# Retention by chunks, its state products inside a projection tile, and attention products in three fp32r parts, in a hybrid decoder step

## The chip, the cores and the metric

The kernel runs on one core of a Trainium2 chip. The metric is the device time of one execution in microseconds, lower is better. The kernel before took 2383.7 us in the median of three runs (2379.57 to 2384.89). The profile comes from one further execution, which took 2381.4 us and whose span is 2379.6 us.

## The reference, cut to what matters

One step of a one-layer decoder on 512 prompt tokens and 8 sample tokens. The width is split in two: 8 heads of attention (keys and values shared by all heads, keys chosen by an indexer) and 8 heads of retention. After them come an output projection and a large MLP. The change touches the two pieces below, for the prompt alone.

```python
# attention, one block of 128 queries; `valid` and the chosen keys are a mask in the kernel
sc = einsum('bqhd,bqkd->bqhk', qq, kg) * ATTN_HEAD_DIM ** -0.5
p = softmax(where(valid, sc, -inf))
out = einsum('bqhk,bqkd->bqhd', p, vg)

# retention, one chunk of n = 128 tokens; R is the state carried from chunk to chunk
def ret_chunk(R, q, k, v, lg):
    decay = where(diff >= 0, exp(diff * lg), 0)
    inner = einsum('bhij,bjhe->bihe', einsum('bihd,bjhd->bhij', q, k) * decay, v)
    cross = einsum('bihd,bhde->bihe', q, R) * exp((i + 1) * lg)
    zeta = exp((n - 1 - i) * lg)
    R_new = exp(n * lg) * R + einsum('bjhd,bjhe,jh->bhde', k, v, zeta)
    return R_new, inner + cross
```

## The kernel before, in words

Everything is held transposed, features on the 128 partitions and the 520 tokens along the row. A projection makes one tile of 128 output features by 520 tokens: 16 blocks of 128 input features, in two units of 8 (`unit`, `tile`, from L637). Weights and activations are split in a high and a low fp32r part, so that each block is three products (high by high, high by low, low by high) on two halves of 260 tokens: 48 matmuls a unit (L647). Plain float32 matmuls are also in use, for the small products.

The engines run programs of their own and meet by semaphores. SP loads the weights, ACT casts them to the high part (`w_hi`, L1070), POOL subtracts to get the low part (`w_lo`, L582), PE multiplies, DVE takes results out of PSUM (accumulator memory). POOL works a few units ahead of PE.

The change lies in the loop over the 8 heads. Each round has four projection tiles: retention values (tile 0), queries (1), keys (2) and gate (3). The attention and retention work of head `i` is written by hand between them on PE:

- in the middle of tile 1 (`values_and_scores`): the values are turned (transposed), and four score blocks `kt,qc` of 128, 256, 384 and 512 keys are made;
- after tile 2: the softmax results `p_h` are turned in 10 blocks; DVE copies them to `pt_h`;
- in the middle of tile 3 (`output_and_decay`): the attention output (`pt_h,vtok`, four matmuls of 512, 384, 256 and 128 columns), the retention scores (`rq,rk`, the same four sizes), and the turned keys;
- after tile 3, in what is called the tail below: the sample products `vbd,ks_tok`, the retention output (`sd_h,vtok_r`, four sizes), the prompt's final state (`vtok_r,ktok`, four of 128 columns), the sample outputs `rq,rs` (eight matmuls of one column), and sums of squares over the features, made by a matmul with a matrix of ones (`rv,ones`, 512 and 8 columns).

Before, the retention is not done chunk by chunk: all 512 by 512 scores of the lower triangle are made and weighed by the decay (L1713).

The small results share four PSUM banks, called `banks`. On PE `fill(e)` gives the bank of the head's result number e, after a wait until result e - 4 has been taken (`s_xd`); on DVE `full(e)` waits until result e is there (`s_xp`). A head has 24 results. The projection tiles have banks of their own, called `product`; a tile may start when the one two tiles back has been taken (`s_evac`).

At the end of a head ACT squares the retention output `ro`, PE sums, ACT takes a square root, and DVE does a Newton step and the gating; this runs beside tile 0 of the next head. In the last head ACT also casts four finished rows of `mix` (the joined head outputs) to `a_hi` right before it squares (L1156, `mixed(0, 4)`), and the output projection follows the loop.

Of the kernel before, what the change touches and what calls it, by code (L numbers as in the profile page):

```python
# [14 lines left out]
P = 128  # L15
D = 2048
KT = D // P
NP_, NS = 512, 8
# [3 lines left out]
NH = 8  # L22
# [39 lines left out]
def unit_of(tile):  # L62

    return 2 * tile
# [59 lines left out]
def build(nc, x_prompt, x_sample, cache_k, cache_v, cache_idx_k, state_ret, page_table, norm1_g, w_in,  # L124
# [3 lines left out]
    with ctx:  # L128
# [72 lines left out]
        for name, shape, dt, nbytes in (  # L201
# [5 lines left out]
            if name == "am":  # L207
                AM_OFFSET = o
            if name == "const":
                assert o >= SMALL + 16384  # L210
# [4 lines left out]
        kit_o = at("kit_o", AM_OFFSET, [P, NP_])  # L215

# [21 lines left out]
        sd_h = at("sd_h", H0, [P, 1280])  # L238
        pt_h = at("pt_h", H0 + 5120, [P, 1280])
# [6 lines left out]
        qc = at("qc", H0 + 15360, [P, NP_])  # L246
# [82 lines left out]
        def pos_stored(pos):  # L329
# [24 lines left out]
         s_th, s_hs, s_head) = (  # L354
# [4 lines left out]
                "ret_sqrt", "head_done"))  # L359
        (s_t1h, s_t1p, s_t1, s_xb, s_n2, s_n2m, s_n2v, s_n2s, s_nf, s_nfm, s_nfv, s_nfs, s_yt,  # L360
         s_yx, s_ye, s_out, s_rn, s_chain) = (
            sem(n) for n in (
                "mixed_hi", "mixed_lo_pool", "mixed_lo", "x_back", "sum2", "sum2_turned", "var2", "sqrt2",
# [271 lines left out]
        def _(pe):  # L635
# [192 lines left out]
            with pe.Fori(0, NH) as i:  # L828
# [5 lines left out]
                e0 = 24 * i  # L834

                def head_tile(u, between=None):
                    tile(m0 + u, TILE_HEAD + u, n0 + 2 * u, unit_of(TILE_HEAD) + 2 * u, between=between)
# [6 lines left out]
                def values_and_scores():  # L844
# [6 lines left out]
                    turn(B[0:NS, fill(1), 0:P], rv[:, NP_:T], P).then_inc(s_xp, 1)  # L851
                    pe.wait_ge(s_qc, i + 1)
                    for b in range(QB):
                        mm(B[:, fill(2 + b), 0:P * (b + 1)], qc[:, b * P:(b + 1) * P], kt[:, 0:P * (b + 1)]
                           ).then_inc(s_xp, 1)

                def output_and_decay():
                    x = fill(10)
                    pe.wait_ge(s_xd, e0 + TAKEN0 + 10)
                    for k in range(QB):  # L860
# [3 lines left out]
                    pe.wait_ge(s_rk, i + 1)  # L864
                    for k in range(QB):
                        mm(B[:, fill(11 + k), 0:NP_ - k * P], rk[:, k * P:(k + 1) * P], rq[:, k * P:NP_]
                           ).then_inc(s_xp, 1)
                    x = fill(15)
# [3 lines left out]
                    turn(B[0:NS, fill(16), 0:P], rk[:, NP_:T], P).then_inc(s_xp, 1)  # L872
# [1242 lines left out]
```

## Time and profile before

| | |
|---|---|
| median of three runs | 2383.7 us |
| the profiled execution | 2381.4 us, span 2379.6 us |
| PE busy | 2319.0 us, 97% of the span |
| DVE busy | 1620.7 us, 68% |
| ACT busy | 912.4 us, 38% |
| POOL busy | 854.7 us, 36% |
| mean granted TensorE clock | 0.989 of full speed |

The busy time of PE is not its speed: matmuls overlap in the records, so a matmul whose row gives 284 ns starts every 120 ns or so. What a product takes is therefore read from the starts of the rows, not from their lengths. A float32 matmul shows as two records in the rows, an fp32r matmul and a turn as one.

### The profile page before, as it was taken

The numbers are of one execution on the slowest core, as the hardware profiler recorded it, in microseconds if no ns is written. First come the engines' busy times: TensorE is split into PE (matmuls) and PEld (weight loads), VectorE is DVE, ScalarE is ACT, GpSimd is POOL, SyncE is SP. The second block draws the span as 40 slices with busy tenths as digits, with TensorE's granted clock in tenths as the row PEclk, the third lists the DMA queues.
The fourth block names the chain that finished last, engine by engine and source line by source line (L and its number), as shares of the span: only waits on it lengthen the run. The fifth ranks groups of instructions, "written<-read, shape, count | busy, mean of one in ns | idle before, by whom it ended". The sixth has DMA issues, their size and how long they took to land.

```text
span 2379.6 us, 46108 instructions
## 1 busy us (share of the span) xinstructions
PE 2319.0 (97%) x18386; PEld 2244.1 (94%) x18386; DVE 1620.7 (68%) x2452; ACT 912.4 (38%) x1180; POOL 854.7 (36%) x355
## 2 busy tenths in 40 slices
PE   8999999999999999999999999999899999999997
PEld 7979899999999899989999999999899999999996
DVE  5358725555555533478888899888877777777775
ACT  5241222222222433355555555555433333333344
POOL 2522322232333444333333333333333333333354
PEclk9999999999999999999999999999999999999998
DMA  6533323333333353425555555566875567655621
GB/s 222 131 80 91 95 63 86 94 85 94 83 81 86 103 178 115 129 74 185 201 199 187 188 191 185 189 201 201 300 256 199 189 210 246 209 185 197 225 97 72
DMA packets 349079, 368.77 MB, mean 155 GB/s; under 512 B 16818, under 2 KB 301682, under 8 KB 348018
## 3 DMA queue, kind: packets, MB, share of 16 engines
q1 hardware_dynamic: 336866, 352.16, 46.5%
q10 hardware_dynamic: 12064, 14.53, 1.7%
q8 instruction: 105, 1.72, 0.3%
q14 instruction: 44, 0.36, 0.1%
HBM read 288.85 MB, written 77.80 MB: 154 GB/s over the span
## 4 chain that ended last, share of the span: by engine, by line
PE 67%; DVE 20%; issue 7%; ACT 4%; DMA 1%; POOL 0%; ACTq 0%; SPq 0%; DVEq 0%; POOLq 0%
PE product L647 30%; PE product L936 29%; DVE banks L1867 7%; PE banks L678 6%; DVE h_lo L1908 4%; ACT w_hi L1249 3%; DVE h_f L1897 2%; DVE w_lo L1873 2%; PE banks L675 1%; DVE c_b L1832 1%; DMA x_in<-in_x_prompt_dram 1%; DVE h_f L1899 1%; DMA w_raw<-in_w_in_dram 1%; ACT h_f L1073 1%; DVE a_lo L1456 0%
## 5 line engine op out<-in xcount | busy, mean ns | idle before, releaser
L615 POOL TENSOR_TENSOR w_lo<-raw,w_hi 128x1024 fp32r<-128x1024 f32 x193 | 495.2, 2566 | 825.5 <-ACT w_hi L1249 825.3
L936 PE MATMUL product<-s_up,w_hi 128*128 128x260 f32 x3600 | 657.4, 284 | 9.0 <-DVE w_lo L1873 5.4
L936 PE MATMUL product<-s_dn,w_hi 128*128 128x260 f32 x3584 | 652.4, 284 | 8.8 <-DVE xr L1975 3.3
L936 PEld LDWEIGHTS product<-s_up,w_hi 128*128 128x128 f32 x3600 | 557.1, 189 | 15.2 <-DVE w_lo L1873 10.5
L936 PEld LDWEIGHTS product<-s_dn,w_hi 128*128 128x128 f32 x3584 | 552.6, 188 | 12.7 <-issue 4.9
L582 POOL TENSOR_TENSOR w_lo<-w_raw,w_hi 128x1024 fp32r<-128x1024 f32 (+1 forms) x134 | 321.8, 2404 | 659.2 <-ACT w_hi L1070 659.0
L936 PE MATMUL product<-s_up,w_lo 128*128 128x260 f32 x1800 | 510.1, 283 | 0.0
L936 PE MATMUL product<-s_dn,w_lo 128*128 128x260 f32 x1792 | 506.9, 283 | 0.0
L647 PE MATMUL product<-a_hi,w_hi 128*128 128x260 f32 (+1 forms) x2144 | 439.6, 286 | 8.9 <-DVE a_lo L1456 3.9
L647 PE MATMUL product<-a_hi,w_lo 128*128 128x260 f32 (+1 forms) x2144 | 433.5, 284 | 0.0
L647 PE MATMUL product<-a_lo,w_hi 128*128 128x260 f32 (+1 forms) x2144 | 432.7, 283 | 0.0
L1249 ACT CAST w_hi<-banks 128x1024 fp32r<-128x1024 f32 x244 | 247.1, 1013 | 452.4 <-DVE banks L1867 342.4
L1873 DVE TENSOR_TENSOR w_lo<-banks,w_hi 128x1024 fp32r<-128x1024 f32 x244 | 297.9, 1221 | 105.5 <-ACT w_hi L1249 105.5
L1070 ACT CAST w_hi<-w_raw 128x1024 fp32r<-128x1024 f32 (+1 forms) x134 | 139.6, 1043 | 555.7 <-PE product L647 414.7
L647 PEld LDWEIGHTS product<-a_hi,w_hi 128*128 128x128 f32 (+1 forms) x2144 | 331.4, 189 | 16.5 <-issue 8.1
L936 PEld LDWEIGHTS product<-s_up,w_lo 128*128 128x128 f32 x1800 | 340.2, 189 | 0.0
L936 PEld LDWEIGHTS product<-s_dn,w_lo 128*128 128x128 f32 x1792 | 336.8, 188 | 0.0
L647 PEld LDWEIGHTS product<-a_hi,w_lo 128*128 128x128 f32 (+1 forms) x2144 | 331.4, 189 | 0.0
L647 PEld LDWEIGHTS product<-a_lo,w_hi 128*128 128x128 f32 (+1 forms) x2144 | 330.3, 188 | 0.0
L1249 ACT CAST w_hi<-raw 128x1024 fp32r<-128x1024 f32 x193 | 203.2, 1053 | 187.5 <-PE product L936 170.3
L1975 DVE TENSOR_TENSOR xr<-xr,product 128x260 f32<-128x260 f32 x416 | 174.5, 420 | 122.7 <-PE product L936 121.2
L1867 DVE TENSOR_TENSOR banks<-raw 128x1024 f32<-128x1024 f32 x118 | 191.9, 1626 | 0.0
(289 smaller groups left out, 1875.6 us busy)
## 6 DMA issues: line engine op xcount, KB each, us to landing
raw<-in_w_up_dram SPq DMA_DIRECT2D x64, 1024.0 KB, 8.4
raw<-in_w_down_dram SPq DMA_DIRECT2D x64, 1024.0 KB, 5.7
s_dn<-hidden_combinations SPq DMA_DIRECT2D x112, 520.0 KB, 8.5
w_raw<-in_w_in_dram SPq DMA_DIRECT2D x100, 512.0 KB, 3.9
hidden_combinations<-h_hi SPq DMA_DIRECT2D x31, 910.0 KB, 3.8
hidden_combinations<-h_lo SPq DMA_DIRECT2D x31, 910.0 KB, 6.6
w_raw<-in_w_out_dram SPq DMA_DIRECT2D x32, 512.0 KB, 4.0
x_transposed<-xr ACTq DMA_DIRECT2D x2, 2080.0 KB, 7.6
```

What stands on the lines that cost most here:

```text
L582: nc.gpsimd.tensor_tensor(w_lo[:, slot, :, 0:cols], w_raw[:, raw, :, 0:cols], w_hi[:, slot, :, 0:cols].bitcast(F32), ALU.subtract).then_in ...
L615: nc.gpsimd.tensor_tensor(ring(w_lo, g, n), block_of(g, i, j), ring(w_hi, g, n).bitcast(F32), ALU.subtract).then_inc(s_lo, 1)
L647: last_mm = nc.tensor.matmul(out[:, half, :], w[:, slot, k, 0:cols], a[:, k0 + k, half * HT:(half + 1) * HT], start=(first and k == 0 and ...
L678: return nc.tensor.matmul(out, lhsT, rhs, start=start, stop=stop, skip_group_check=True)
L936: mm_last = nc.tensor.matmul(out, w[:, k, col:col + P], s[:, h, k, :], start=(first and k == 0 and part == 0), stop=(last and k == kn - 1 ...
L1070: nc.scalar.copy(w_hi[:, n % RING, :, 0:cols], w_raw[:, n % 2, :, 0:cols]).then_inc(s_hi, 1)
L1249: nc.scalar.copy(ring(w_hi, g, n), x).then_inc(s_hi, 1)
L1867: v.tensor_tensor(out, x, y, ALU.add).then_inc(s_t, 1)
L1873: v.tensor_tensor(ring(w_lo, g, n), sums_in(g, (k + 1) % 2), ring(w_hi, g, n).bitcast(F32), ALU.subtract).then_inc(s_lt, 1)
L1897: v.tensor_tensor(h_f[:, 5, :], h_f[:, 0, :], a21[:, :], ALU.subtract)
L1908: v.tensor_tensor(low[:, :, :], h_f[:, :, :], high[:, :, :].bitcast(F32), ALU.subtract).then_inc(s_hl, 1)
L1975: ins = v.tensor_tensor(acc, acc, part, op)
```

## The change

Four things are changed in the head loop, and one before it.

1. The attention scores and outputs are each made of three fp32r matmuls (high by high, high by low, low by high) instead of one float32 matmul. The parts of the shared keys and values are made once, before the loop (four DVE operations, of which the last two wait until the values have been stored). The parts of the queries are made by DVE in each head (`qc`, `qc_lo`). Of the turned probabilities ACT makes the high part from PSUM and DVE the low part (`pt_lo`); before, DVE made one copy.
2. Retention is done by chunks: four score blocks of 128 columns in one bank, one decay multiplication, and for chunks 1 to 3 a second matmul with the state carried so far (`carry`) on decayed queries (`rqd`).
3. The products for the states are no longer in the tail. They are kept apart by chunk, and go in before block 14 of the 16 of tile 3 (`partial_states`), with the sample products `vbd,ks_tok`. DVE then makes the carried states and the final state from them.
4. On DVE the sample states `rs` are updated before the gate tile is taken, not after. A head now has 20 results in the banks. The small sum of the sample squares goes to the bank of the sample outputs.

```diff
@@ PE
                     for b in range(QB):
-                        mm(B[:, fill(2 + b), 0:P * (b + 1)], qc[:, b * P:(b + 1) * P], kt[:, 0:P * (b + 1)]
-                           ).then_inc(s_xp, 1)
+                        x, rows_, keys = fill(2 + b), slice(b * P, (b + 1) * P), slice(0, P * (b + 1))
+                        for part, (q, k) in enumerate(((qc, kt_hi), (qc_lo, kt_hi), (qc, kt_lo))):
+                            last = mm(B[:, x, keys], q[:, rows_], k[:, keys], start=(part == 0), stop=(part == 2))
+                        last.then_inc(s_xp, 1)
...
                     for k in range(QB):
-                        last = mm(B[:, x, k * P:NP_], vtok[:, k, :], pt_h[:, KOFF[k]:KOFF[k] + NP_ - k * P],
-                                  start=(k == 0), stop=(k == QB - 1))
+                        for part, (values, probs) in enumerate(((vtok_hi, pt_h), (vtok_hi, pt_lo), (vtok_lo, pt_h))):
+                            last = mm(B[:, x, k * P:NP_], values[:, k, :], probs[:, keys],
+                                      start=(k == 0 and part == 0), stop=(k == QB - 1 and part == 2))
...
                     for k in range(QB):
-                        mm(B[:, fill(11 + k), 0:NP_ - k * P], rk[:, k * P:(k + 1) * P], rq[:, k * P:NP_]
-                           ).then_inc(s_xp, 1)
+                        last = mm(B[:, x, k * P:(k + 1) * P], rk[:, k * P:(k + 1) * P], rq[:, k * P:(k + 1) * P])
+                    last.then_inc(s_xp, 1)
...
+                def partial_states(k):
+                    if k != 14:
+                        return
+                    x = fill(14)
+                    pe.wait_ge(s_xd, e0 + TAKEN0 + 14)
+                    for c in range(QB):
+                        last = mm(B[:, x, c * P:(c + 1) * P], ktok[:, c, :], vtok_r[:, c, :])
+                    last.then_inc(s_xp, 1)
+                    pe.wait_ge(s_vbd, i + 1)
+                    for j in range(2):
+                        mm(B[:, fill(15 + j), :], ks_tok[:, :], vbd[:, 4 * j:4 * j + 4, :]).then_inc(s_xp, 1)
...
+                head_tile(3, between=output_and_decay, ready=partial_states)
+                x = fill(17)
                 for k in range(QB):
-                    last = mm(B[:, x, k * P:NP_], vtok_r[:, k, :], sd_h[:, KOFF[k]:KOFF[k] + NP_ - k * P],
-                              start=(k == 0), stop=(k == QB - 1))
+                    out = B[:, x, k * P:(k + 1) * P]
+                    last = mm(out, vtok_r[:, k, :], sd_h[:, k * P:(k + 1) * P], stop=(k == 0))
+                    if k:
+                        if k == 1:
+                            pe.wait_ge(s_cq, i + 1)
+                        pe.wait_ge(s_sc1, 3 * i + k)
+                        last = mm(out, carry[:, k - 1, :], rqd[:, (k - 1) * P:k * P], start=False)
@@ ACT
                 high(base + 5, i8)
+                for k in range(QB):
+                    n = NP_ - k * P
+                    act.wait_ge(s_xp, 20 * i + 7 + k)
+                    nc.scalar.copy(pt_h[:, KOFF[k]:KOFF[k] + n], B[:, (6 + k) % 4, 0:n]).then_inc(s_pth, 1)
                 act.wait_ge(s_rq, i + 1)
@@ DVE
+                full(9)
                 for k in range(QB):
-                    n = NP_ - k * P
-                    v.tensor_copy(pt_h[:, KOFF[k]:KOFF[k] + n], B[:, full(6 + k), 0:n]).then_inc(s_xd, 1)
+                    n = slice(KOFF[k], KOFF[k] + NP_ - k * P)
+                    dve.wait_ge(s_pth, 4 * i + k + 1)
+                    v.tensor_tensor(pt_lo[:, n], B[:, (6 + k) % 4, 0:NP_ - k * P], pt_h[:, n].bitcast(F32),
+                                    ALU.subtract).then_inc(s_xd, 1)
...
-                for k in range(QB):
-                    v.tensor_tensor(sd_h[:, KOFF[k]:KOFF[k] + n], B[:, full(11 + k), 0:n], dh[:, 0:n], ALU.mult
-                                    ).then_inc(s_xd, 1)
+                v.tensor_tensor(sd_h[:, :].rearrange("p (k d) -> p k d", d=P),
+                                B[:, full(11), :].rearrange("p (k d) -> p k d", d=P),
+                                dh[:, 0:P].unsqueeze(1).to_broadcast([P, QB, P]), ALU.mult).then_inc(s_xd, 1)
...
-                scaled(halves(rg[:, :]), m0 + 3, (TILE_HEAD + 1) % 2)
+                v.tensor_tensor(rqd[:, :], rq[:, P:NP_], dh[:, P:NP_], ALU.mult).then_inc(s_cq, 1)
+                x = full(14)
+                v.tensor_scalar(carry[:, 0, :], B[:, x, 0:P], st[:, 45:46], None, ALU.mult).then_inc(s_sc1, 1)
+                for k in range(1, QB - 1):
+                    dve.wait_ge(s_sc1, 3 * i + k)
+                    v.scalar_tensor_tensor(out=carry[:, k, :], in0=B[:, x, k * P:(k + 1) * P], scalar=st[:, 45:46],
+                                           in1=carry[:, k - 1, :], op0=ALU.mult, op1=ALU.add).then_inc(s_sc1, 1)
+                dve.wait_ge(s_sc1, 3 * i + 3)
+                v.scalar_tensor_tensor(out=rst[:, :], in0=carry[:, QB - 2, :], scalar=st[:, 37:38],
+                                       in1=B[:, x, (QB - 1) * P:NP_], op0=ALU.mult, op1=ALU.add).then_inc(s_xd, 1)
                 dve.wait_ge(s_rs, 16 * i + 16)
...
+                scaled(halves(rg[:, :]), m0 + 3, (TILE_HEAD + 1) % 2)
+                v.tensor_copy(ro[:, 0:NP_], B[:, full(17), :]).then_inc(s_xd, 1)
```

Two places of the order matter most. The first is PE's tail, from the end of tile 3 to the sum of squares. Before it stands so:

```order
L647 MATMUL product<-a_hi,w_lo 128x260 x2
L841 REGISTER_ALU [waits values_diagonal]
...
L678 MATMUL banks<-vbd,ks_tok 128x512 [waits head_bank_taken]
...
L678 MATMUL banks<-sd_h,vtok_r 128x512 [waits head_bank_taken]
L678 MATMUL banks<-sd_h,vtok_r 128x384
L678 MATMUL banks<-sd_h,vtok_r 128x256
L678 MATMUL banks<-sd_h,vtok_r 128x128
...
L678 MATMUL banks<-vtok_r,ktok 128x128 x3
...
L678 MATMUL banks<-rq,rs 128x1 x7
...
L678 MATMUL banks<-rv,ones 128x512 [waits head_bank_taken,ret_squared]
```

In the changed kernel the same stretch, from the last blocks of tile 3 on (`vtok_r,ktok` are the state products, now in the middle of tile 3's second unit, and `rqd,carry` the products with the carried states):

```order
L692 MATMUL banks<-vtok_r,ktok 128x128 [waits head_bank_taken]
L692 MATMUL banks<-vtok_r,ktok 128x128 x3
L856 REGISTER_ALU [waits values_diagonal]
...
L692 MATMUL banks<-vbd,ks_tok 128x512 [waits head_bank_taken]
L661 MATMUL product<-a_hi,w_hi 128x260 x2
...
L692 MATMUL banks<-sd_h,vtok_r 128x128
L926 ISA [waits ret_q_decayed]
L692 MATMUL banks<-rqd,carry 128x128 [waits states_carried]
L692 MATMUL banks<-sd_h,vtok_r 128x128
...
L692 MATMUL banks<-rqd,carry 128x128 [waits states_carried]
...
L692 MATMUL banks<-rq,rs 128x1 x7
...
L692 MATMUL banks<-rv,ones 128x512 [waits head_bank_taken]
```

The sample products and the state products have moved ahead of the last two blocks of tile 3 (six matmuls each), and the sums of squares are the last thing in the tail as before, behind the sample outputs `rq,rs`.

The second place is DVE, from the sample values `vbd` to the retention output, where `rg` is the gate tile, `rs` the sample states and `ro` the retention output. Before:

```order
L1719 TENSOR_TENSOR vbd<-vs_tok,const 72x1024
...
L1476 TENSOR_TENSOR rg<-product,rb 128x520 [waits weights_used]
...
L1725 SCALAR_TENSOR_TENSOR rs<-rs,st,banks 128x512 [waits head_bank_full]
...
L1725 SCALAR_TENSOR_TENSOR rs<-rs,st,banks 128x512 [waits head_bank_full]
...
L1728 COPY ro<-banks 128x512 [waits head_bank_full]
...
L1729 COPY rst<-banks 128x128 [waits head_bank_full]
...
L1730 COPY ro<-banks 128x8 [waits head_bank_full]
```

And in the changed kernel:

```order
L1769 TENSOR_TENSOR vbd<-vs_tok,const 72x1024
L1771 TENSOR_TENSOR rqd<-rq,dh 128x384
...
L1773 TENSOR_SCALAR carry<-banks,st 128x128 [waits head_bank_full]
...
L1776 SCALAR_TENSOR_TENSOR carry<-banks,st,carry 128x128 [waits states_carried]
...
L1776 SCALAR_TENSOR_TENSOR carry<-banks,st,carry 128x128 [waits states_carried]
...
L1779 SCALAR_TENSOR_TENSOR rst<-carry,st,banks 128x128 [waits states_carried]
...
L1784 SCALAR_TENSOR_TENSOR rs<-rs,st,banks 128x512 [waits head_bank_full]
...
L1784 SCALAR_TENSOR_TENSOR rs<-rs,st,banks 128x512 [waits head_bank_full]
...
L1512 TENSOR_TENSOR rg<-product,rb 128x520 [waits weights_used]
...
L1788 COPY ro<-banks 128x512 [waits head_bank_full]
```

The gate tile was first in DVE's queue at the end of tile 3; now five small operations and the two updates of the sample states stand ahead of it, and the copy of `ro` stands behind it.

## Rows read from the trace of the kernel before

**Rows 1.** The page, busy time and share of the span of each engine.
```profile
PE 2319.0 (97%) x18386; PEld 2244.1 (94%) x18386; DVE 1620.7 (68%) x2452; ACT 912.4 (38%) x1180; POOL 854.7 (36%) x355
```

**Rows 2.** Chain of waits, 430 to 520 us: start us, us, what, matmul records.
```profile
449.69 17.57 PE product L647 x144
...
468.49 1.92 PE banks L678 x4
...
494.59 4.31 PE banks L678 x16
498.90 0.55 PE banks L675 x5
...
505.23 6.28 PE banks L678 x38
...
511.57 8.54 PE product L647 x69
```

**Rows 3.** PE's timeline, a tail: start us, us, engine, line, operation, output<-inputs, records.
```profile
505.06 0.62 PE L678 MATMUL banks<-vbd,ks_tok 72*128 72x512 f32 x2
505.52 2.32 PE L678 MATMUL banks<-sd_h,vtok_r 128*128 128x512 f32 x8
507.68 1.06 PE L678 MATMUL banks<-vtok_r,ktok 128*128 128x128 f32 x8
508.57 1.84 PE L678 MATMUL banks<-rq,rs 128*128 128x1 f32 x16
510.28 1.23 PE L678 MATMUL banks<-rv,ones 128*128 128x512 f32 x4
```

**Rows 4.** Timeline of PE's weight loads at the scores, in brackets the wait.
```profile
467.54 0.53 PEld L678 LDWEIGHTS banks<-kt,qc 128*128 128x128 f32 x4
468.49 0.30 PEld L678 LDWEIGHTS banks<-kt,qc 128*128 128x128 f32 x2 [0.42 <-DVE vtok_r L1688]
469.28 0.30 PEld L678 LDWEIGHTS banks<-kt,qc 128*128 128x128 f32 x2 [0.50 <-DVE vs_tok L1660]
```

**Rows 5.** Timeline of DVE, ACT and POOL in a tail, in brackets the wait.
```profile
443.95 1.40 DVE L1725 SCALAR_TENSOR_TENSOR rs<-rs,st,banks 128x512 f32<-128x512 f32 x2
...
444.45 2.36 POOL L582 TENSOR_TENSOR w_lo<-w_raw,w_hi 128x1024 fp32r<-128x1024 f32 x1 [8.21 <-ACT w_hi L1070]
...
445.95 0.69 DVE L1728 COPY ro<-banks 128x512 f32<-128x512 f32 x1 [0.60 <-PE banks L678]
...
446.67 0.63 ACT L1073 ACTIVATE rv<-ro 128x512 f32<-128x512 f32 x1 [1.76 <-DVE ro L1728]
446.84 0.29 DVE L1729 COPY rst<-banks 128x128 f32<-128x128 f32 x1 [0.20 <-PE banks L678]
...
448.52 0.17 DVE L1730 COPY ro<-banks 128x8 f32<-128x8 f32 x1 [1.39 <-PE banks L678]
```

**Rows 6.** Timeline of ACT, POOL and DVE in tile 3, up to `vbd`.
```profile
488.82 1.19 ACT L1165 COPY t<-product 64x520 f32<-64x520 f32 x2
488.88 2.40 POOL L582 TENSOR_TENSOR w_lo<-w_raw,w_hi 128x1024 fp32r<-128x1024 f32 x1 [3.29 <-ACT w_hi L1070]
...
490.67 1.17 DVE L1679 SCALAR_TENSOR_TENSOR t<-t,cs 128x520 f32<-128x520 f32 x1
...
500.89 1.22 DVE L1719 TENSOR_TENSOR vbd<-vs_tok,const 72x1024 fp32r<-72x1024 f32 x1
```

**Rows 7.** Timeline of ACT and PE in the last head's tail.
```profile
815.98 0.62 PE L678 MATMUL banks<-vbd,ks_tok 72*128 72x512 f32 x2
...
817.72 2.19 ACT L1156 CAST a_hi<-mix 128x520 fp32r<-128x520 f32 x4
...
821.19 1.23 PE L678 MATMUL banks<-rv,ones 128*128 128x512 f32 x4
```

**Rows 8.** Busy us (count) of each engine by stretch, then the granted clock of PE.
```profile
573.00:574.00 1.00, 0.92 (x7) 0.79 (x7) 0.70 (x3) 0.40 (x1) 0.00 (x0) 0.95 0.23 66
574.00:575.00 1.00, 1.00 (x6) 1.00 (x6) 0.67 (x2) 0.99 (x2) 0.00 (x0) 0.50 0.83 269
```

More of the change, by code:

```diff
@@ L829, in _, with head_tile @@
                 m0, n0 = TILE_HEAD + 4 * i, unit_of(TILE_HEAD) + 8 * i
-                e0 = 24 * i
-                def head_tile(u, between=None):
-                    tile(m0 + u, TILE_HEAD + u, n0 + 2 * u, unit_of(TILE_HEAD) + 2 * u, between=between)
+                e0 = 20 * i
+                def head_tile(u, between=None, ready=None):
+                    tile(m0 + u, TILE_HEAD + u, n0 + 2 * u, unit_of(TILE_HEAD) + 2 * u, between=between,
+                         ready=ready)
                 def fill(e):
@@ L883, in _ @@
                     last.then_inc(s_xp, 1)
[L884 to L900 removed]
+                head_tile(3, between=output_and_decay, ready=partial_states)
+                x = fill(17)
+                for k in range(QB):
+                    out = B[:, x, k * P:(k + 1) * P]
[5 more added lines that the diff above has]
+                        last = mm(out, carry[:, k - 1, :], rqd[:, (k - 1) * P:k * P], start=False)
+                last.then_inc(s_xp, 1)
+                x = fill(18)
+                pe.wait_ge(s_xd, e0 + TAKEN0 + 17)
                 for b in range(NS):
@@ L1196, in act_head @@
                     mixed(4, 5)
[L1197 removed]
+                act.wait_ge(s_xd, 20 * i + TAKEN0 + 20)
+                act.wait_ge(s_vt, i + 1)
                 act_fn(rk[:, :], rv[:, :], ACT.Sqrt).then_inc(s_hs, 1)
@@ L1661, in split_thirds @@
                 return last
+            v.tensor_copy(kt_hi[:, :], kt[:, 0:NP_]).then_inc(s_kv, 1)
+            dve.wait_ge(s_kv, 1)
+            v.tensor_tensor(kt_lo[:, :], kt[:, 0:NP_], kt_hi[:, :].bitcast(F32), ALU.subtract).then_inc(s_kv, 1)
+            dve.wait_ge(s_kvo, 64)
+            v.tensor_copy(vtok_hi[:, :, :], vtok[:, :, :]).then_inc(s_kv, 1)
+            dve.wait_ge(s_kv, 3)
+            v.tensor_tensor(vtok_lo[:, :, :], vtok[:, :, :], vtok_hi[:, :, :].bitcast(F32), ALU.subtract
+                            ).then_inc(s_kv, 1)
             v.memset(ks_tok[:, :].bitcast(F32), 0.0)
             step(v.memset(vs_tok[:, :].bitcast(F32), 0.0))
-            with step.loop(NH, 14) as i:
-                m0, e0 = TILE_HEAD + 4 * i, 24 * i
+            with step.loop(NH, 15) as i:
+                m0, e0 = TILE_HEAD + 4 * i, 20 * i
                 def full(e):
@@ L1685, in _ @@
                 step(v.tensor_copy(st[:, 41:42], gamma[:, one(i)]))
-                v.tensor_copy(qc[:, :], row(qa, i)[:, 0:NP_]).then_inc(s_qc, 1)
+                step(v.reciprocal(st[:, 45:46], st[:, 37:38]))
+                v.tensor_copy(qc[:, :], row(qa, i)[:, 0:NP_]).then_inc(s_qch, 1)
+                dve.wait_ge(s_qch, i + 1)
+                v.tensor_tensor(qc_lo[:, :], row(qa, i)[:, 0:NP_], qc[:, :].bitcast(F32), ALU.subtract
+                                ).then_inc(s_qc, 1)
                 scaled(halves(rv[:, :]), m0, TILE_HEAD % 2)
```

79 lines of the change are left out of this document (41 added, 38 removed).

## The prediction, made before the changed kernel was run

> **What bounds the kernel now.** I read the page first: PE is busy for 97% of the span and DVE for 68% [rows 1]. Then the chain of waits over one head, because the whole change lies in the eight rounds of that loop. The chain is PE alone: from tile 0's start at 449.69 to the next one at 511.57, 61.88 us a head, and none of the listed pieces is another engine's [rows 2]. So a microsecond taken from PE's stream is a microsecond of the kernel, as long as no other engine becomes late; and the work put on ACT and DVE is free only as far as it is ready when PE comes to it. Starts in PE's timeline give what each product takes [rows 3], the waits before the weight loads show the two places where PE already stands still for DVE [rows 4], and DVE's, ACT's and POOL's timelines give the durations for the new chains [rows 5, 6].
>
> **The unit prices.** The projection has 144 matmuls of 260 columns in 17.57 us [rows 2], 0.122 us each. The fp32r pair of 512 columns runs from 505.06 to 505.52, 0.23 us each [rows 3]. The float32 product of four sizes (1280 columns) runs from 505.52 to 507.68, 2.16 us; four float32 matmuls of 128 columns from 507.68 to 508.57, 0.89 us, 0.222 each, 0.111 a record; one-column matmuls 16 records from 508.57 to 510.28, 0.107 a record [rows 3]. That last row says that a record with almost no columns still takes 0.107 us: the weights have to be loaded. I take that as the floor of a 128-column fp32r matmul: 0.113 us.
>
> **Part 1, attention in three parts.** No row shows fp32r under 260 columns. My values for one fp32r matmul: 128 columns 0.113 (the floor), 256 0.120 (as 260), 384 0.172 (between 260 and 512), 512 0.23. Three of each: 3 x 0.635 = 1.90 us, against 2.16 before. Output: -0.26 us a head. By size it is a loss at 128 columns (0.34 against 0.22) and a gain from 256 up. From above, a 128-column one could cost what a float32 one does, 0.222: +0.33 us a head on the output. From below 0.056, half a float32 record (128 columns at the rate of the 512): -0.17.
> The Trainium skill ("TensorE: Matmul & The Clock Gate", LDWEIGHTS) has a load of P columns at P/1.2 ns, 107 ns for 128, which speaks against cutting into 128-column pieces; the one-column row agrees (107). The same page (Back-to-back issue gap) has N/2.4 + 2.5 ns for an isolated matmul, 56 ns at 128 columns; an estimate by that alone makes the three-part set 1.63 us and the kernel about 2 us faster than I say. At 260 columns it has 111 ns against 122 measured, so I stay with the rows.
> The scores gain less, because PE stands there for DVE: 0.42 us for the values and 0.50 for `vs_tok` before the last, 512-column block, whose load starts at 469.28 [rows 4]. These ends don't move, and the first three blocks lie before them, so only the last block counts: four passes of 512 columns take 2.16 x 512/1280 = 0.86 us, three fp32r 0.69: -0.17 us a head.
> The new operations beside it: ACT's four copies to the high part go ahead of the half swap (488.82) [rows 6]. ACT takes 0.63 for 512 columns [rows 5], about 1.9 for the four; the swap then ends near 491.9. DVE's four subtractions follow the copies and end near 491.6, the rotation of the keys ends near 494.6. PE wants the probabilities at 494.4 and the rotated keys behind the 1.9 us of the output, at 496.3. Both hidden, with 1.7 us to spare at the narrower place. The query split (0.7 us more on DVE at a head's start) lies ahead of taking tile 0, and PE wants that tile only a unit later, 48 x 0.122 = 5.9 us. The splits before the loop have the whole of tile 0, 11.7 us.
>
> **Part 2, retention by chunks.** The scores: 0.89 for 2.16, -1.27 us a head. The second half: before, output 2.16 and state 0.89, 3.05 together; after, state products 0.89 and seven matmuls of 128 columns, 1.55, together 2.44: -0.61 us a head. On DVE one multiplication of 512 columns (0.69) takes the place of four.
>
> **Part 3, the states inside tile 3.** Taking them out of the tail makes nothing cheaper on PE; it changes who is late. PE reaches block 14 some 4.3 us (36 matmuls) after the turned keys, 7.6 us after the start of the output. DVE has by then, counted from that start: the attention output 2.1 to 2.8, the decay to 3.7, `ktok` to 4.4, three small splits to 5.3, `vbd` (1.22 [rows 6]) to 6.6, `rqd` to 7.2. So PE finds everything there, with 1 us to spare. One more change between fp32r and float32 is new: I give it 0.1 us, half of what lies between the sums' work (510.28 plus 0.86 and 0.21) and tile 0's start at 511.57 [rows 2, 3]. Bounds 0 to 0.3.
>
> **Part 4, the tail.** Let S be the start of the state products. They end at S + 0.89, `vbd` at S + 1.35, tile 3 at S + 2.9. DVE: three carries and the final state at 0.29 each (a 128-column copy [rows 5]) with some 0.17 between, to S + 2.8; two updates of `rs`, 1.40 [rows 5], to S + 4.15; the gate tile, 0.70, to S + 4.85; the copy of `ro`, 0.69, to S + 5.5. ACT: tanh to S + 5.5, square 0.63 to S + 6.2. PE: seven matmuls to S + 4.45, the sample outputs 1.71 to S + 6.16, and then it wants the squares. So the square, which was ready 1 us early (446.67 + 0.63 [rows 5], against 510.28 less a period [rows 3]), is now just late: +0.1 us a head. Bounds -0 and +0.7.
>
> **The sum for heads 1 to 7.** -0.26 - 0.17 - 1.27 - 0.61 + 0.1 + 0.1 = -2.1 us; times 7: -14.8 us. Every period should go from 61.9 to 59.8.
>
> **The last head.** ACT has four casts, 2.19 us, between tanh and square [rows 7]. Before they lay beside 6.3 us of tail. Now tanh ends 2.6 us after tile 3, the casts at 4.8, the square at 5.5, where PE is there at 3.3. The sum of squares starts 5.5 after the tile's end; before, it was 5.2 (821.19 less 815.98, where the sample products begin [rows 7]). The tail gains nothing, and what the middle gains (1.27 + 0.26 + 0.17) is used up by the state products moved into it (1.35) and the 0.1. About 0 for this head, where 2.1 would be expected.
>
> **The total.** 2381.4 - 14.8 = 2366.6 us for the profiled execution. The median lies 2.3 above that execution, which gives 2368.9. I take 2368. Everything after the loop stays bound by PE and only starts earlier.
>
> **The rivals.**
> *The clock.* After one of the eight tails the granted clock fell from 1.00 to 0.50 (2.4 to 1.2 GHz) for some 3.4 us, behind the one-column matmuls and the sums [rows 8]; half of that, 1.7 us, is lost. For it: the tail keeps its thinnest piece and gets a short stand still. Against: its other pieces are as dense as they were, and seven tails went by undisturbed. If it happens after most tails, six more, +10 us: 2378, a gain of about 0.2%. Chance 8%.
> *Small fp32r matmuls at float32's price.* If both 128 and 256 columns, the sizes below any row, cost as float32 (0.222 and 0.43), one set takes 3 x (0.222 + 0.43 + 0.172 + 0.23) = 3.16 us. The output loses 1.0 instead of gaining 0.26; at the scores the first three blocks now pass the waits and the loss is about 0.55. The head's gain falls to 0.1 us, the last head loses 1.5: 2382, no change. For it: no row excludes it. Against: the rate is flat between 260 and 512. Chance 6%. With 128 columns alone at that price it is 2.6 us: 2371, within my range.
> *Slower: the gate tile and the copy of `ro` behind POOL.* A DVE operation on two SBUF operands stands still while POOL works: the rotation's second step, 1.17 us for 520 columns, ends 0.56 after POOL's `w_lo` does (490.67 + 1.17 against 488.88 + 2.40) [rows 6]. POOL's `w_lo` runs from 1.3 to 3.7 us after tile 3's end (444.45 to 446.81 [rows 5], the end being 505.06 less a period). Before, the gate tile was done by then; now it lies in the middle of it (from 1.25 to 1.95). If it is held till POOL ends, it ends at 4.3, the square at 5.8, and PE waits 2.5 us in each head: 7 x 2.4 and as much in the last, +19 us: 2387, slower. It decides from a delay of 2.1 us a head. Against: two updates of `rs`, which like the gate tile read one PSUM and one SBUF operand, ran in the same POOL operation at 0.70 us each (1.40 for two, POOL from 444.45) [rows 5]. Chance 4%.
> *The move backfires at block 14.* If DVE is some 2 us late with `vbd`, PE stands in the middle of tile 3. POOL's hold could put 1.7 us on `vbd` or `rqd`, of which 1 us is covered: +0.7 a head, 2374. Chance 8%.
>
> **How the numbers follow.** The forecast 2368 has 70%, with an own range of 2363 to 2374 from the bounds above (-1.4 and +2.6 for small fp32r matmuls, up to +4 for the tail's wait, two clock falls of 1.7 either way, the run's own spread). The others: clock 8, block 14 8, small matmuls 6, POOL 4, and 4 left for what I don't see, on the slow side. The range for 8 in 10 is 2361 to 2376. Within 0.2% (4.8 us) of 2383.7 is what a measurement of this kernel cannot tell from no change: faster, under 2378.9, 0.85; same 0.09; slower 0.06.
>
> **What would show it.** The chain should still be PE alone, with starts of tile 0 59.8 us apart; 0.89 us between the first retention score and the turned keys; 1.9 us for the twelve output matmuls (2.3 would mean float32's price at 128 columns); no wait at block 14; the sum of squares starting 3.3 to 3.4 us after tile 3's end in seven heads and about 5.5 in the last, with the wait put down to ACT. I am wrong if PE's product starts in the tail or at block 14 are more than 0.5 us later than this, or if the clock falls after more than two tails.

## The result, and the profile after

The changed kernel took 2364.03 us (median of four runs, 2361.38 to 2365.37); the kernel before, run beside it, 2382.83 us (2379.57 to 2384.89). The ratio is 0.9922, with a 95% interval of 0.991 to 0.9935: 18.8 us faster, a little under 0.8%. The forecast was 2368, the range 2361 to 2376. The profiled execution took 2365.37 us (span 2363.6, mean granted clock 0.986, against 2379.6 and 0.989 before).

The page of the kernel after, busy time of each engine (it answers to [rows 1]):

```profile
PE 2304.8 (98%) x18498; PEld 2253.6 (95%) x18498; DVE 1630.9 (69%) x2480; ACT 922.2 (39%) x1212; POOL 853.5 (36%) x355
```

PE has 112 more records and is busy for 14 us less; DVE is busy for 10 us more. Next the chain of waits of the kernel after over one period and a half (start us, us, what, matmul records), which answers to [rows 2]:

```profile
428.58 5.78 PE product L661 x48
434.37 2.80 PE banks L692 x20
...
437.71 4.34 PE product L661 x36
442.05 1.35 PE banks L692 x10
443.40 1.44 PE product L661 x12
444.84 4.33 PE banks L692 x34
...
449.19 19.07 PE product L661 x144
...
510.24 9.87 PE product L661 x80
```

Over this stretch it is still PE alone. Output and retention scores take 2.80 us where they took 4.31, the tail's chain piece 4.33 where it took 6.28, and the state products stand inside tile 3 as 1.35 (442.05). From 449.19 to 510.24 there are 61.05 us, but tile 0 took 19.07 there instead of 17.57: the clock had fallen. Undisturbed periods, as from 510.24 to the next tile 0 at 569.73, are 59.5 us; before they were 61.9. That is 2.4 us a head, where I said 2.1.

The sum of the profiled execution: from the first tile 0 to the end of the last sum of squares it was 498.1 us (324.16 to 822.27) and is 482.9 (327.67 to 810.59), 15.2 less. Seven heads at 2.4 would be 16.8 and the last head's middle 0.4, 17.2 together; 2.0 are missing, nearly all of it the clock's part: the last sum of squares ran at half clock (1.1) and more of the first tile did (0.8). The loop began 3.5 us later, with more half clock ahead of it. What follows it took 4.3 less (1557.3 and 1553.0 us), though its code is the same; in the profiled execution of experiment 9 the same code took 1556.5, so I don't count these 4.3 as the change's. The two profiled executions differ by 16.0 us and the medians by 18.8; no row shows where the other 2.8 come from.

The prices of the new products stand in PE's timeline of the kernel after (start us, duration us, engine, line, operation, output<-inputs, records; durations overlap, so the starts are read):

```profile
434.20 0.39 PE L692 MATMUL banks<-pt_h,vtok_hi 128*128 128x512 f32 x1
...
434.90 0.34 PE L692 MATMUL banks<-pt_h,vtok_hi 128*128 128x384 f32 x1
...
435.43 0.28 PE L692 MATMUL banks<-pt_h,vtok_hi 128*128 128x256 f32 x1
...
435.78 0.22 PE L692 MATMUL banks<-pt_h,vtok_hi 128*128 128x128 f32 x1
...
436.06 1.10 PE L692 MATMUL banks<-rq,rk 128*128 128x128 f32 x8
```

512 columns take 0.235 us each (434.20 to 434.90 for three), 384 take 0.177, 256 take 0.117 and 128 take 0.093 (the starts of this last group are uneven; experiment 7 prices it better); the set is 1.86 us, where I had 1.90 and float32 took 2.16 [rows 3].

The tail of the kernel after, DVE, ACT, POOL and PE in one timeline (in brackets the wait), which answers to [rows 5]:

```profile
444.40 1.40 DVE L1784 SCALAR_TENSOR_TENSOR rs<-rs,st,banks 128x512 f32<-128x512 f32 x2
...
444.68 0.60 PE L692 MATMUL banks<-sd_h,vtok_r 128*128 128x128 f32 x4
...
445.72 0.69 DVE L1512 TENSOR_TENSOR rg<-product,rb 128x520 f32<-128x520 f32 x1
...
446.00 2.36 POOL L596 TENSOR_TENSOR w_lo<-w_raw,w_hi 128x1024 fp32r<-128x1024 f32 x1 [8.02 <-ACT w_hi L1101]
...
446.24 1.84 PE L692 MATMUL banks<-rq,rs 128*128 128x1 f32 x16
...
447.17 0.63 ACT L1104 ACTIVATE rv<-ro 128x512 f32<-128x512 f32 x1
...
447.95 1.23 PE L692 MATMUL banks<-rv,ones 128*128 128x512 f32 x4
```

Tile 3 ends at 444.68. The square is done at 447.80 and PE takes it at 447.95, without a wait: 3.27 us after tile 3's end, as forecast (3.3 to 3.4). The copy of `ro` (446.44) lies wholly beside POOL's operation, the gate tile with its last 0.4 us, and each takes 0.69 us, so POOL holds neither.

Behind this tail the clock fell. The stretches of the kernel after (busy us and count of each engine, then PE's granted clock), as [rows 8] of before:

```profile
449.00:450.00 1.00, 0.98 (x7) 0.89 (x6) 0.91 (x3) 0.07 (x1) 0.00 (x0) 0.73 0.35 102
450.00:451.00 1.00, 1.00 (x7) 1.00 (x6) 0.46 (x1) 1.00 (x1) 0.00 (x0) 0.50 0.89 291
```

About 3.4 us at 0.50 (1.2 of 2.4 GHz), of which half, 1.7, would be lost; the period shows 1.5 of it (61.05 against 59.5). It happened after one of the seven tails, as before.

### The profile page after: what moved, and what is told of

It is laid out like the page before. It is cut to its first block, busy times and chain, and to the rows that moved or that the text cites. A ratio compares the mean times of both kernels' runs of the same rounds, so it can differ in the third digit from the quotient of the medians.

```text
span 2363.6 us, 46420 instructions
## 1 busy us (share of the span) xinstructions
PE 2304.8 (98%) x18498; PEld 2253.6 (95%) x18498; DVE 1630.9 (69%) x2480; ACT 922.2 (39%) x1212; POOL 853.5 (36%) x355
## 4 chain that ended last, share of the span: by engine, by line
PE 67%; DVE 21%; issue 7%; ACT 4%; DMA 1%; POOL 0%; DVEq 0%; SPq 0%; ACTq 0%
PE product L661 32%; PE product L967 28%; DVE banks L1927 7%; PE banks L692 5%; DVE h_lo L1968 4%; ACT w_hi L1285 3%; DVE w_lo L1933 2%; DVE h_f L1957 2%; PE banks L689 1%; DVE c_b L1892 1%; DMA x_in<-in_x_prompt_dram 1%; DVE h_f L1959 1%; ACT h_f L1104 1%; DVE s_up L1874 1%; DVE h_f L1958 0%
```

## The experiments

All edits are to the kernel after. "Seven tails" are those of heads 1 to 7. The kernel before, run beside them, had medians of 2381.4 to 2382.6 us.

**1. Attention in float32 (part 1 undone).**

```
- for part, (q, k) in enumerate(((qc, kt_hi), (qc_lo, kt_hi), (qc, kt_lo))):
-     last = mm(B[:, x, keys], q[:, rows_], k[:, keys], start=(part == 0), stop=(part == 2))
+ mm(B[:, x, keys], qc[:, rows_], kt[:, keys]).then_inc(s_xp, 1)
  (the output product likewise, with vtok and pt_h in float32; ACT's copies and DVE's splits go)
```

> The changed kernel with the attention scores and outputs as single float32 matmuls again (no parts of keys, values, queries and probabilities, no ACT copies). My theory: part 1 is worth 0.26 us a head on the output and 0.17 on the scores, so the head's period goes from 59.5 us to 59.9 and the kernel is 3 to 4 us slower than the changed one (about 2367). Rival, small fp32r pieces are dear: no change or a gain. Rival, the extra gain that I didn't foresee comes from this part: 6 us or more slower.

Measured: 2367.69 us (2364.76 to 2375.96), ratio 0.9946 [0.9931, 0.9961]. Its chain of waits:

```profile
446.48 17.51 PE product L661 x144
...
491.30 3.05 PE banks L692 x16
...
506.36 8.75 PE product L661 x71
```

A period of 59.88 to 59.9 us, 0.4 more than after: output and retention scores 3.05 against 2.80 (0.25; I had 0.26), the rest at the scores. Part 1, undone alone, is worth 0.4 us a head; the other 2.0 are with parts 2 to 4.

**2. State products in the tail (the move undone).**

```
- head_tile(3, between=output_and_decay, ready=partial_states)
+ head_tile(3, between=output_and_decay)
+ partial_states()
```

> The changed kernel with the state products and the sample products behind tile 3 again, everything else as it is. Theory: the move makes nothing cheaper on PE but hides DVE's chain (carries, final state, sample states, gate tile, copy of ro) behind two blocks of tile 3. Without it PE reaches the sample outputs 2.9 us after tile 3's end, the sample states are ready at 4.0, the squares at 6.1 where PE is there at 5.8: 1.5 us a head more than the changed kernel, period 61.0, some 11 us slower in all (about 2375), about what the kernel before took less the attention part and a third of the chunking. Rival, the move is neutral because DVE is not late: within 2 us of the changed kernel.

Measured: 2386.92 us (2378.58 to 2393.5), ratio 1.0026 [1.0013, 1.004]: slower than the kernel before, 22 us above after, where I expected half of that. PE in two of its tails, and its waits from 380 to 800 us (us in total, times, longest):

```profile
571.14 1.95 PE L692 MATMUL banks<-rq,rs 128*128 128x1 f32 x16 [0.89 <-DVE rs L1783]
...
631.79 1.96 PE L692 MATMUL banks<-rq,rs 128*128 128x1 f32 x16 [0.89 <-DVE rs L1783]
```

```profile
PE banks L692 <- DVE rs L1783: 6.2, 7, 0.9
```

The one-column products, which need the updated `rs`, stand 0.9 us for DVE in every tail. And the clock fell after five of seven tails. A stretch of another of its tails:

```profile
511.00:512.00 1.00, 1.00 (x2) 0.48 (x3) 0.14 (x1) 0.21 (x1) 0.00 (x0) 0.50 0.00 0
```

From one tail to the next, a period without a fall is 60.65 us (571.14 to 631.79), 1.1 above after, of which the stand is 0.9; I had expected 61.0. A period with a fall is 62.2 (508.94 to 571.14). So seven heads cost about 8 us by the waits. The profiled execution was the fastest of the seven, only 13.2 us above the profiled one of after; in the others the clock was lower still. Over all runs the mean granted clock was 0.9816, against 0.9870 in after, and 0.0054 of 2385 us is 13 us: an estimate, which with the 8 makes 21 of the 22.9.

**3. Gate tile first in the tail (part 4's order undone).**

```
+ scaled(halves(rg[:, :]), m0 + 3, (TILE_HEAD + 1) % 2)
  for j in range(2):
      (the two updates of rs)
- scaled(halves(rg[:, :]), m0 + 3, (TILE_HEAD + 1) % 2)
```

> The changed kernel with the gate tile taken before the two updates of the sample states, as in the kernel before. Theory: DVE then waits with the updates for tile 3's end (gate tile to 0.9 us after it, updates to 2.3), and PE, which comes to the sample outputs 1.56 us after tile 3, stands 0.8 us in each head: period 60.3, some 5 to 6 us slower (about 2369.5). Rival, the tail of the changed kernel is bound by the squares on ACT: tanh is done earlier here, so the squares come no later and nothing changes.

Measured: 2379.31 us (2376.18 to 2384.71, 12 runs), ratio 0.9991 [0.9982, 0.9999]. 15 us given back, not 5 or 6. PE's product in the first tail, then the timeline of the second and its clock:

```profile
384.83 1.95 PE L692 MATMUL banks<-rq,rs 128*128 128x1 f32 x16 [0.54 <-DVE rs L1785]
...
443.09 0.70 DVE L1512 TENSOR_TENSOR rg<-product,rb 128x520 f32<-128x520 f32 x1 [0.40 <-PE product L661]
443.70 1.40 DVE L1785 SCALAR_TENSOR_TENSOR rs<-rs,st,banks 128x512 f32<-128x512 f32 x2
...
445.15 2.17 PE L692 MATMUL banks<-rq,rs 128*128 128x1 f32 x16 [0.54 <-DVE rs L1785]
```

```profile
445.00:446.00 1.00, 0.84 (x8) 0.85 (x8) 0.70 (x2) 0.27 (x1) 1.00 (x1) 1.00 0.00 0
...
447.00:448.00 1.00, 1.00 (x3) 0.67 (x4) 0.17 (x1) 0.21 (x1) 0.00 (x0) 0.50 0.00 0
```

The gate tile waits 0.40 us for PE and then runs ahead of the updates; the one-column products stand 0.54 us, and 1.6 us later the clock goes to half. It fell after six of seven tails, and once stayed down for twice the 3.4 us. The one period before any of these falls is 60.32 us (384.83 to 445.15), just the 60.3 that I had expected, 0.8 more than after. The periods that hold one fall are 61.7 to 61.8. So what I missed is the clock. 15.3 us are 2.2 a head: with the falls behind it, a stand of half a microsecond costs four times its length. All runs have that clock, not only the profiled one: 0.9833 in the mean against 0.9870, some 9 us by the same estimate.

**4. Both undone (states in the tail, gate tile first).** Edits 2 and 3 together: with them nothing of the new order is left, only the cheaper products.

> The changed kernel without part 3: state and sample products behind tile 3 and the gate tile first in DVE's queue there, as before the change. Chunking and the three-part products stay. Theory: PE stands about 1.0 us for the sample states and nothing or 0.2 for the squares, as with the late gate tile, and the clock falls after most tails (1.7 us each). Period 61.1 without such a fall; 2380 to 2388 in all, so that the whole gain of parts 1 and 2 is eaten. Rival, with the gate tile first the chain is short enough: under 2372.

Measured: 2381.67 us (2379.61 to 2388.28, 11 runs), ratio 1.0004 [0.9995, 1.0013]. The wait from 380 to 800 us:

```profile
PE banks L692 <- DVE rs L1784: 6.3, 7, 0.9
```

0.9 us in each tail, and the clock fell after all seven, so that there is no period without a fall to read; with one it is 62.1 us. The mean clock of all runs was 0.9824. Without the new order the whole gain of the cheaper products is gone: what PE saves turns into a wait for DVE and a slower clock.

**5. The last head: a quarter of the casts ahead of the squares, the rest behind.**

```
- mixed(0, 4)
+ mixed(0, 1)
  (the squares)
+ if last: mixed(1, 4)
```

> The changed kernel with one cast of mix ahead of the squares in the last head and the other three behind them. Theory: PE stood 1.75 us there and its clock fell to half for 3.4 us behind it; with one cast the wait is 0.6 us, the clock stays, POOL (busy until 3.7 us after the tile) starts its eight subtractions no later, and DVE's subtractions start 2 to 3 us earlier, which takes away the 1.8 us wait of the output projection for a_lo. 2 us faster than the changed kernel (about 2362). Rival: the output projection is bound by POOL's eight subtractions, and nothing is gained: within 0.5 us. The seven other heads must not move.

Measured: 2363.51 us (2358.77 to 2368.01), ratio 0.9925 [0.9911, 0.9939], the same as after; the times alone cannot tell a gain of 2 us from one of 0.5. PE in its last tail, then its waits from 330 to 860 us:

```profile
804.67 1.24 PE L692 MATMUL banks<-rv,ones 128*128 128x512 f32 x4 [0.17 <-ACT rv L1104]
```

```profile
PE product L661 <- POOL a_lo L619: 3.5, 8, 0.7
```

The stand for ACT goes from 1.8 us to 0.2, and no clock fall follows. But PE then reaches the out projection sooner and waits 3.5 us, in eight pieces, for POOL's subtractions for `a_lo`. The last wait of PE for DVE's `a_lo` ends 2.33 us earlier than in after (827.61, 829.94), but the tail's one-column products start 2.19 us earlier too (802.65, 804.84), so the edit gained 0.1 there. The rival was right: the wait moves to the next engine.

**6. An extra copy of a 260-column PSUM block on DVE, ahead of the gate tile.**

```
+ v.tensor_copy(qc[:, 0:HT], G[:, 2 * ((TILE_HEAD + 1) % 2), 0:HT])
  scaled(halves(rg[:, :]), m0 + 3, (TILE_HEAD + 1) % 2)
```

> The changed kernel with one extra copy on DVE (260 columns out of PSUM, 0.42 us, its result is used by nobody) ahead of the gate tile. It doses the delay of the squares. In the changed kernel the square ends 0.15 us before PE wants it, so PE should stand 0.25 to 0.3 us in each tail. Theory A, only the wait counts: period 59.5 to 59.8, 2 to 2.5 us slower than the changed kernel. Theory B, what made the two earlier undone orders so slow is the granted clock, which falls after a tail in which PE stands still: then more than one of the seven tails should be followed by half clock, at 1.7 us each, and the kernel is 5 to 12 us slower. I hold B.

Measured: 2367.46 us (2364.26 to 2368.61), ratio 0.9935 [0.9921, 0.9949]. Its chain:

```profile
570.32 17.37 PE product L661 x144
...
629.83 10.20 PE product L661 x84
```

59.51 us, as after, though the copy takes 0.42 us of DVE. The sum of squares starts 0.2 us later, but tile 0 behind it takes 17.37 instead of 17.55, so that the period gives it back. I had thought that the tail had nearly no slack; a delay of 0.4 us costs nothing in the period. The median is 3.4 us above after all the same. One more fall (1.5 us) and a longer stand in the last head (2.09 us for 1.75) are part of it; the rest no row shows. Two of seven tails were followed by half clock, with only 0.2 us of stand ahead of the squares, so this run does not decide between theories A and B.

**7. Output pieces of 64 columns.** The last 128-column piece of the output as two of 64, six matmuls for three.

> The changed kernel with the 128-column piece of the attention output made as two pieces of 64 columns, so six fp32r matmuls for three. Theory: a small fp32r matmul costs its weight load, 0.107 to 0.113 us, whatever its columns; the set takes 0.32 us more (2.18 for 1.86). Rival, it costs its columns: the set stays within 0.05 us.

Measured: 2371.53 us, one run. Its chain:

```profile
571.62 17.57 PE product L661 x144
...
616.34 3.14 PE banks L692 x23
...
631.44 8.62 PE product L661 x70
```

Period 59.82, 0.3 more; the piece of output and scores 3.14 us against 2.80, 0.34 for three more matmuls: 0.11 each. A matmul of 64 columns costs what one of 128 does, and a one-column record 0.107 us [rows 3]: the columns don't set the price there. That it is the weight load is the reading that fits; no run took the load away.

**8. The block of `vs_tok` given back after two of its three reads** (the third copy reads the SBUF copy).

```
- split_thirds(vs_tok, B[0:NS, full(1), 0:P], ("hi", "lo", "hi")).then_inc(s_xd, 1)
+ step(v.tensor_copy(vs_tok[0:NS, :], x))
+ v.tensor_tensor(vs_tok[THIRDS[1]:...], x, vs_tok[0:NS, :]..., ALU.subtract).then_inc(s_xd, 1)
+ step(v.tensor_copy(vs_tok[THIRDS[2]:...], vs_tok[0:NS, :]...))
```

> The changed kernel, and on DVE the bank with the sample values is given back after two of its three reads; the third copy reads the SBUF result. Theory: PE stands 0.32 us for this bank before the 512-column score block; the release comes 0.3 us earlier, of which the end of the block before allows 0.15 to 0.2. Period 59.5 to 59.3, 1 to 1.5 us faster than the changed kernel. Rival, the next wait (the bank of the first result) takes its place and nothing moves.

Measured: 2360.89 us (2358.96 to 2365.84), ratio 0.9913 [0.99, 0.9927]; the periods are 59.2 us. Its chain over one head:

```profile
403.61 2.15 PE banks L692 x12
405.76 17.27 PE product L661 x144
...
444.72 17.55 PE product L661 x144
...
464.96 5.13 PE product L661 x43
```

The first tile behind the scores starts 59.20 us later (405.76, 464.96) and the scores are 2.15 us, where after they were 1.46 and 0.96 with a wait of 0.32. That wait is gone and 0.3 us a head is won, some 2 us in seven heads; the wait of 0.19 us one block earlier stays. By the medians this is 3 us under after, but the runs' own spread is as large.

**9. A stand of 0.7 us elsewhere.** PE waits behind tile 2 of each head for an extra DVE copy that can start only when that tile is done.

```
  head_tile(2)
+ pe.wait_ge(s_stand, i + 1)
```

> The changed kernel with a stand of PE of about 0.7 us in each head, but away from the tail: after tile 2 PE waits until DVE has copied 260 columns out of that tile's PSUM (a result nobody uses). It tells apart what lowers the clock in the orders whose tails have a wait of 0.5 to 0.9 us. Theory: a short stand does it only beside the thin one-column matmuls of the tail; here the seven heads cost 0.7 us each and no more of them than one or two are followed by half clock: about 2370. Rival: any stand of that length does it; then most heads show half clock behind tile 2, 1.7 us each, and the kernel takes about 2380.

Measured: 2374.67 us (2368.18 to 2375.27), ratio 0.9958 [0.9944, 0.9973]. The stand, and the clock behind it:

```profile
548.30 1.30 PE L689 MATMUL banks<-const,p_h 128*128 128x128 f32 x10 [0.71 <-DVE qc L1755]
```

```profile
549.00:550.00 1.00, 1.00 (x11) 1.00 (x10) 0.32 (x1) 1.00 (x3) 1.00 (x1) 1.00 0.00 0
```

The clock stayed at 1.00 behind all of these stands; it fell after two of the seven tails. The period without a fall is 60.45 us, 0.95 more. So a stand of 0.7 us among dense matmuls costs its length and some 0.2; one of 0.54 us beside the one-column matmuls cost 1.7 us beyond its length (experiment 3). That period is nearly the 60.32 us of experiment 3, so a longer way from tail to tail isn't what lowers the clock there. The median is 10.6 us above after, of which eight periods give 7.6; in the profiled execution the code behind the loop took 3.5 us more.

**10. Scores from the largest block down, with edit 8.**

```
- for b in range(QB):
+ for j, b in enumerate(reversed(range(QB))):
```

> The early release of the sample values' bank, and the four score blocks in the order 512, 384, 256, 128 keys instead of 128 to 512 (on PE, DVE and ACT alike). Theory: the two waits of PE for DVE there (0.19 and 0.32 us a head in the changed kernel) lie behind the small blocks because these are too short to cover DVE's copy; with the big blocks first both waits are covered, the stretch falls from 2.43 to about 1.9 us, the period from 59.5 to 58.95, and the kernel is 4 to 5 us faster than the changed one, some 2 faster than the early release alone. Rival: DVE's softmax steps on the big blocks come late for the third and fourth and the waits only move: the same as the early release alone.

Measured: 2363.06 us (2358.29 to 2365.55), ratio 0.992 [0.9907, 0.9934]. Its chain:

```profile
403.90 1.87 PE banks L692 x12
405.77 17.37 PE product L661 x144
...
444.83 5.19 PE product L661 x41
```

The twelve score matmuls take 1.87 us, with no wait left. The period is 59.05 us; of the 0.28 won at the scores against edit 8, the next 144 matmuls give back 0.1. The medians don't tell this kernel from after or from edit 8: it is 1 us under after, where I expected 4 to 5. By the period it is the best of all, 2.9 us a head under the kernel before.

## Why the prediction was right, point by point

**PE alone is the bound, so its saving is the kernel's.** Right, but under a condition that I gave too little weight (below). That the loop's sums nearly agree, -14.8 forecast and -15.2 in the profile, is partly luck: each of seven heads gained 0.3 more than I said (2 us), and the half clock in the first tile and in the last sum of squares took 1.9 back.

**Part 1.** Output forecast -0.26 a head, measured 0.25 by experiment 1. Scores -0.17: the stretch went from 2.60 to 2.43 us, as forecast, because only the block behind the last wait counted. The waits at the scores became 0.19 and 0.32 us [rows 4: 0.42 and 0.50]; the ends did not move. The price at 128 columns (0.113 us) holds: experiment 7 gives 0.11. The formula for an isolated matmul in the Trainium skill ("TensorE: Matmul & The Clock Gate", Back-to-back issue gap) would have made the output set 1.63 us, an estimate; 1.86 were measured, and the measurement decides. With these 1.86 the rival of small matmuls at float32's price falls too, since it has 3.16.

**Part 2.** Forecast -1.27 at the retention scores; with the output -1.53, measured 4.31 - 2.80 = 1.51.

**Parts 2 to 4, the tail.** This is the term of the sum that was mis-sized. Forecast, the state products' 1.4 in tile 3 included: -0.61 + 0.1 + 0.1 = -0.41 a head. Measured, from tile 3's end to the next tile 0: 6.51 us before (505.06 to 511.57 [rows 2, 3]) and 4.51 after (444.68 to 449.19), with 1.35 more in tile 3: -0.65. Neither of my two tenths came. The second unit of tile 3 with the states inside is 4.34 + 1.35 + 1.44 = 7.13 us, and 48 matmuls without them are 5.78 in the same chain (428.58), so nothing is paid for changing from fp32r to float32 and back. And the square was in time, since DVE's operations followed one another more closely than the 0.17 us that I put between them: the gate tile ended at 446.41, 1.73 after tile 3's end, where I had 1.95. The rest of the 2.4, 0.06 a head, lies in the projection's tiles.

**The last head.** Forecast 0, with the sum of squares about 5.5 us after the tile's end, put down to ACT. Measured, in PE's timeline of the kernel after:

```profile
808.44 2.29 PE L692 MATMUL banks<-rv,ones 128*128 128x512 f32 x4 [1.75 <-ACT rv L1104]
```

It starts 5.16 us after the tile's end at 803.28. Up to that end the head is 0.4 us shorter than before, which its middle gives. The clock fell at this stand, and the sum of squares took 2.15 us instead of 1.08: from tile 0 to its end the head is 0.6 longer. That one us is on the path, since DVE's normalization starts from that sum. So the forecast of 0 was 0.6 us off, by a clock fall that it did not have.

**The rivals.** *The gate tile behind POOL*: it did not happen, by the tail shown above. *Block 14 backfires*: it did not; `vbd` was done at 440.5 and `rqd` at 441.0, PE came at 441.89 without a wait. *The clock*: in this kernel no, one fall in seven tails as before. But it is the closest of the rivals, and I gave it 8% by the wrong argument, that the tail's pieces are as dense as they were. What the runs show to matter is whether PE stands beside the one-column products. The stands there and the falls behind them, over all kernels, with the mean granted clock of all runs of each:

```
kernel                       stand at rq,rs   falls in 7 tails   mean clock
before, after                0                1, 1               0.988, 0.987
1, 5, 6, 7, 8, 10            0                2, 1, 2, 0, 1, 0   0.986 to 0.988
9 (0.7 us elsewhere)         0                2                  0.987
3 gate tile first            0.54             6                  0.983
2 states in the tail         0.89             5                  0.982
4 both                       0.9              7                  0.982
```

Experiment 3 is the cleanest of them: PE's own order is that of after, and only the stand is new. The eighth tail says the same. In ten of the twelve kernels PE stands there for half a microsecond or more, before `rq,rs` or between them and the sums of squares, 1.75 us in after, and the clock fell there in all ten; in the other two, before and experiment 5, it stands 0 and 0.17 us and the clock stayed.

Without the move of the state products and the order of the tail the kernel is 17.6 us slower (experiment 4 against after), nearly the whole 18.8 of the change, though they make nothing cheaper on PE. In the prediction I wrote of the move that it makes nothing cheaper and only changes who is late. That was right, and its size was missing: shortening PE's work in that head without it makes DVE 0.9 us late, and the clock more than doubles the bill: by the mean clocks (0.9824 and 0.9870) some 11 of the 17.6 us are its part, an estimate.

**What stays open.** Why the clock still falls after one or two tails in kernels without a stand. Falls come in rows there too, 61.4 us apart (686.6 and 748.0 us in experiment 1), so one may make the next likelier; no run tests that. How the falls grow with the stand is not known either: no kernel here had one between 0 and 0.54 us at `rq,rs`. Experiment 2 costs 5 us more than experiment 4, although it has fewer falls in its profiled execution; that one was its fastest of runs that spread over 15 us. Its mean clock over all runs is slightly lower (0.9816 against 0.9824, 2 us), and its squares come 0.14 us later in each tail, 1 us in all. The rest is not explained.

## What to carry to other kernels

When a change takes time from the bounding engine, look at the nearest operation that now waits for another engine, and at what stands there: a stand beside matmuls that stream few columns can cost several times its length through the clock; here a stand among dense ones cost about its length. Move work of the bounding engine into that gap before ordering the other engine's queue more cleverly, and then order the queue by who is waited for first. Don't price short matmuls by their columns; read the price from a one-column row of the trace.

## What the runs showed of the hardware

- The granted clock fell from 1.00 to 0.50 some 1.6 to 3.2 us after the end of stands of 0.54 us beside one-column matmuls (six of seven, experiment 3), stayed there for 3.4 us or twice that, and did not fall behind stands of 0.71 to 0.80 us among matmuls of 128 to 260 columns (none of eight, experiment 9).
- An fp32r matmul with its own weights: 512 columns 0.235 us, 384 0.177, 256 0.117, 128 and 64 0.11 (experiment 7). At 128 columns three fp32r matmuls cost more than one float32 matmul (0.33 against 0.222 [rows 3]); sizes between 128 and 256 were not run.
- POOL's `w_lo` (446.00 to 448.36) left DVE's operation with one PSUM and one SBUF operand at 0.69 us. In experiment 5 DVE's operations on two SBUF operands or one, beside POOL's `a_lo`, took 1.68 and 1.40 us; the same two took 0.70 and 0.43 in after, where POOL was done by then. Not every one is held so long: the operation ahead of them, also on two SBUF operands beside POOL, took 0.87. Such rows in DVE's and POOL's timeline of that experiment:

```profile
804.78 11.48 POOL L619 TENSOR_TENSOR a_lo<-mix,a_hi 128x520 fp32r<-128x520 f32 x8
...
813.43 1.68 DVE L1472 TENSOR_TENSOR rq<-rq,rk 128x520 f32<-128x520 f32 x1
815.14 1.40 DVE L1473 TENSOR_SCALAR rq<-rq 128x520 f32<-128x520 f32 x1
816.58 0.70 DVE L1474 TENSOR_TENSOR rk<-rk,rq 128x520 f32<-128x520 f32 x1
```
